# Local attention scores in stage 2: from one float32 product over 64 rows to two bf16 products over 128 rows, and silu with a bounded exponent

## The chip, the cores and the metric

The kernel runs on one core of a Trainium2 chip. The metric is the device time of one execution in microseconds, as the median of several runs. The profile is of one execution of its own. Engines are named as in the profile: PE (TensorE, with PEld for its weight loads), DVE (VectorE), ACT (ScalarE), POOL (GpSimd) and SP (SyncE, which issues the DMAs here).

## The reference

The program computes a block with gated linear attention, and on its result a second layer with three branches: an mLSTM branch, a local attention branch and a stick-breaking branch. Each branch is multiplied by silu of a gate. The change concerns the silus of the second layer and the scores of its local attention. Cut to that, the reference is:

```
def swa_branch(q, k, v, sinks):            # A_HEADS = 6, A_KV = 2, A_DH = 64, WINDOW = 128
    ...
    qb = q.reshape(B, nb, WINDOW, A_KV, G, A_DH)          # G = 3 query heads per key head
    kh = k.reshape(B, nb, WINDOW, A_KV, A_DH)
    kk = jnp.concatenate([jnp.concatenate([pad, kh[:, :-1]], 1), kh], 2)   # block before, own block
    scores = jnp.einsum('bnqkgd,bnskd->bnkgqs', qb, kk).astype(jnp.float32) * (A_DH ** -0.5)
    ...
    probs = jax.nn.softmax(jnp.concatenate([scores, sink], axis=-1), axis=-1)[..., :-1]

def hybrid_layer(...):
    h = rmsnorm_2(x, g_pre) * (1.0 + scale[:, None]) + shift[:, None]
    (mu, mv, mi, mf, mz, aq, ak, av, az, sq, sk, sv, sz) = jnp.split(h @ w_in, OFFSETS, axis=-1)
    y_m = mlstm_branch(mu, mv, ...) * jax.nn.silu(mz)     # with silu(causal_conv(u)) inside
    y_a = swa_branch(aq, ak, av, a_sinks) * jax.nn.silu(az)
    y_s = stickbreak_branch(sq, sk, sv) * jax.nn.silu(sz)
    ...
```

## The kernel before

The program has three stages. Stage 1 computes the first layer, 16 tiles of 128 tokens. Stage 2 (`mix_phase`) computes, for the same 16 tiles in order, the projections of the second layer, its mLSTM branch and its local attention, and writes the operands of the stick-breaking branch to memory. Stage 3 (`stick_phase`) computes that branch, the output product and the norm. Between stages all engines meet.

In stage 2 each engine runs its own list of instructions, written out by hand in the function `tile` of its block. Engines wait for each other by semaphores whose names say what is done (`aqk_done`, `aqk_copied`, `h_lo_done`). An engine works through its list in the order in which it is written; nothing is rearranged. The order of the lists and the PSUM bank that a product goes to therefore set all the timing.

The projections are float32 products in three bf16 ones: high times high, high times low, low times high (lines L1413, L1414, L1415). For tile i PE does in order: the forget and input gates and u (bank G0), mz (G1), then queries and keys `aq`, `ak` (G0, which must have been emptied of u by ACT, `u_copied`), the transposes of the probabilities and heads of tile i-1, v (G1), small products that turn the gate rows into columns (L1507 to L1510) and spread a row over 128 partitions (L1514, into bank B7, which DVE must have read for the heads of tile i-1, `ym_mid`), az (G0, which needs `aqk_copied`), the probabilities of tile i-1 times v (L1468), q and k of the mLSTM (L1528, L1529), sq and sk (G1), the mLSTM's own products, sz (G0), sv (G1), the intra-tile product (L1568) and last the scores of the local attention (L1584): 6 heads by 2 blocks of keys (one block in the first tile), each a float32 product over 64 rows, 128 queries by 128 keys. Then the next tile's gate products wait for `h_lo_done`.

ACT empties the banks. For each silu it copies the product to `z_sb` and takes the exponential of its negative to `e_sb` (`gate_out`, L1145 and L1146). When the last of the three, sz, is there, it takes the logarithm of 1 + e and the exponential of its negative over all 1024 columns (L1210, L1211). That is released as `silu_rec` to POOL, which multiplies it with `z_sb` (L1118). ACT goes on with the copy of sv (L1214) and the high half of the next tile's h (L1140, `h_hi_done`); DVE makes the low half (L1257, `h_lo_done`). DVE then goes straight on: numerators and denominators of the mLSTM (L1364 to L1373), scores plus bias (L1381), their maxima (L1385 to L1388). ACT takes the exponentials of the scores (L1229) and then, first in its list of the next tile, copies u out of G0 (L1165).

For the scores ACT copies the queries, scaled, and the keys as float32 from bank G0 (L1177, L1178). Keys of two tiles are kept. POOL computes the causal convolution with nine instructions (L1088 to L1094) and DVE in the same time the row chain of the gates with nine small ones (L1310 to L1319). The silu of the convolution is again three passes of ACT (L1183 to L1185) and a multiplication by DVE (L1327). In stage 1, ACT computes the silu of c for the second layer once, in its first tile (L352 to L356).

## Time and profile before

| | us |
|---|---|
| median of 3 runs | 2326.86 (2325.99 to 3398.17) |
| profiled execution, its own time | 2321.77 |
| its span | 2320.0 |

| engine | busy in the span | share |
|---|---|---|
| PE | 2118.8 us | 91% |
| DVE | 1422.6 us | 61% |
| ACT | 1111.8 us | 48% |
| POOL | 567.5 us | 24% |

Stage 1 takes the first 946 us or so, stage 2 the time to about 1770, stage 3 the rest. The shares are averages over the three stages; in stage 2 alone PE is busy nearly all the time. A matmul's record is longer than the time until the next one starts, so the cost of a row of products is read from start to start. On ACT and DVE, too, an instruction that waits for nothing can start before the record of the last one ends. A row in brackets says how long the engine was idle before it and who ended that.

### The profile page before, as it was taken

The numbers are of one execution on the slowest core, as the hardware profiler recorded it, in microseconds if no ns is written. First come the engines' busy times: TensorE is split into PE (matmuls) and PEld (weight loads), VectorE is DVE, ScalarE is ACT, GpSimd is POOL, SyncE is SP. The second block draws the span as 40 slices with busy tenths as digits, with TensorE's granted clock in tenths as the row PEclk, the third lists the DMA queues.
The fourth block names the chain that finished last, engine by engine and source line by source line (L and its number), as shares of the span: only waits on it lengthen the run. The fifth ranks groups of instructions, "written<-read, shape, count | busy, mean of one in ns | idle before, by whom it ended". The sixth has DMA issues, their size and how long they took to land. (4 is left out here: it accounts for less than half of the span.)

```text
span 2320.0 us, 48214 instructions
## 1 busy us (share of the span) xinstructions
PE 2118.8 (91%) x19996; PEld 1488.3 (64%) x19996; DVE 1422.6 (61%) x2478; ACT 1111.8 (48%) x2407; POOL 567.5 (24%) x554
## 2 busy tenths in 40 slices
PE   1699999999999998699999999999994698989887
PEld 1466666666666664599988999998992343434333
DVE  6755555555555553256665555666554798989885
ACT  2444444444444443234434334434333687978775
POOL 0520100000000100333343333344332232323221
PEclk9799999999999998899999999999996899999999
DMA  9422222223222224411001011001004312020111
GB/s 398 151 89 81 84 80 76 88 90 102 81 89 85 89 71 141 131 26 46 27 27 30 27 29 46 27 27 30 27 18 155 109 46 82 23 88 19 64 55 55
DMA packets 129962, 174.54 MB, mean 75 GB/s; under 512 B 46928, under 2 KB 98256, under 8 KB 127696
## 3 DMA queue, kind: packets, MB, share of 16 engines
q1 hardware_dynamic: 129456, 170.41, 22.8%
q8 instruction: 158, 2.59, 0.5%
q10 hardware_dynamic: 288, 1.05, 0.1%
q14 instruction: 60, 0.49, 0.1%
HBM read 122.39 MB, written 49.03 MB: 74 GB/s over the span
## 5 line engine op out<-in xcount | busy, mean ns | idle before, releaser
L1413 PE MATMUL m_bank<-h_hi,w_all 128*128 128x128 bf16 (+1 forms) x2560 | 437.5, 220 | 19.2 <-POOL m_arena L1041 17.7
L1415 PE MATMUL m_bank<-h_hi,w_all 128*128 128x128 bf16 (+1 forms) x2560 | 436.9, 220 | 0.1
L1414 PE MATMUL m_bank<-h_lo,w_all 128*128 128x128 bf16 (+1 forms) x2560 | 436.9, 220 | 0.0
L1413 PEld LDWEIGHTS m_bank<-h_hi,w_all 128*128 128x128 bf16 (+1 forms) x2560 | 251.5, 98 | 27.8 <-POOL m_arena L1041 18.2
L1414 PEld LDWEIGHTS m_bank<-h_lo,w_all 128*128 128x128 bf16 (+1 forms) x2560 | 251.7, 98 | 0.6 <-issue 0.2
L1415 PEld LDWEIGHTS m_bank<-h_hi,w_all 128*128 128x128 bf16 (+1 forms) x2560 | 251.7, 98 | 0.0
L1774 POOL TENSOR_TENSOR s_hi<-s_sp,s_cols 128x512 bf16<-128x512 f32 x144 | 152.3, 1057 | 352.9 <-DVE s_sp L1869 141.2
L283 POOL TENSOR_TENSOR g_stage<-g_stage,g_nh_row 128x1024 f32<-128x1024 f32 x16 | 52.3, 3272 | 736.0 <-DVE g_stage L617 736.0
L680 PE MATMUL g_bank<-w_all,h_hi 128*128 128x512 bf16 x512 | 194.2, 379 | 0.7 <-ACT g_stage L372 0.7
L681 PE MATMUL g_bank<-w_all,h_hi 128*128 128x512 bf16 x512 | 194.0, 379 | 0.0
L682 PE MATMUL g_bank<-w_all,h_lo 128*128 128x512 bf16 x512 | 194.0, 379 | 0.0
L680 PE MATMUL g_bank<-h_hi,w_all 128*128 128x128 bf16 x1024 | 175.3, 220 | 0.0
L681 PE MATMUL g_bank<-h_lo,w_all 128*128 128x128 bf16 x1024 | 175.1, 220 | 0.0
L682 PE MATMUL g_bank<-h_hi,w_all 128*128 128x128 bf16 x1024 | 175.0, 220 | 0.0
L1795 ACT ACTIVATE s_ar<-s_ar 128x512 f32<-128x512 f32 x144 | 89.6, 622 | 69.7 <-DVE s_ar L1880 69.6
L1942 PE MATMUL s_bank<-s_q,s_k_c 128*128 128x256 bf16 x576 | 89.6, 281 | 26.9 <-issue 13.7
L1880 DVE TENSOR_TENSOR s_ar<-s_zs,s_bank 128x512 f32<-128x512 f32 x144 | 98.4, 683 | 24.1 <-PE s_bank L1960 22.1
L1968 PE MATMUL s_bank<-s_ar,s_v_c 128*64 128x256 f32 x576 | 94.8, 408 | 14.0 <-ACT s_ar L1795 13.3
L1875 DVE TENSOR_TENSOR s_lo<-s_sp,s_hi 128x512 bf16<-128x512 f32 x144 | 99.2, 689 | 12.9 <-POOL s_hi L1774 12.9
L1791 ACT ACTIVATE s_ab<-s_ab,s_cols 128x512 f32<-128x512 f32 x144 | 104.2, 723 | 4.7
L680 PEld LDWEIGHTS g_bank<-h_hi,w_all 128*128 128x128 bf16 x1024 | 100.8, 98 | 1.8 <-issue 0.2
L1864 DVE SCALAR_TENSOR_TENSOR s_sp<-s_zs,s_ab 128x512 f32<-128x512 f32 x144 | 98.8, 686 | 3.7 <-ACT s_ab L1791 1.4
(349 smaller groups left out, 5295.8 us busy)
## 6 DMA issues: line engine op xcount, KB each, us to landing
g_piece<-in_w_dram SPq DMA_DIRECT2D x64, 268.0 KB, 3.3
g_stage<-in_gla_w_in_dram SPq DMA_DIRECT2D x8, 1552.0 KB, 12.4
g_stage<-in_ada_w_dram SPq DMA_DIRECT2D x8, 1536.0 KB, 11.3
g_piece<-in_w_mod_t_dram SPq DMA_DIRECT2D x48, 256.0 KB, 3.2
w_hi<-g_piece_hi SPq DMA_DIRECT2D x64, 134.0 KB, 2.0
w_lo<-g_piece_lo SPq DMA_DIRECT2D x64, 134.0 KB, 2.2
g_xs<-in_x_dram SPq DMA_DIRECT2D x16, 512.0 KB, 4.3
s_xr<-x SPq DMA_DIRECT2D x16, 512.0 KB, 4.1
```

Source lines behind the costliest of these rows:

```text
L680: pe.matmul(out, l_hi, r_hi, start=(k == 0), stop=False)
L681: pe.matmul(out, l_hi, r_lo, start=False, stop=False)
L682: ins = pe.matmul(out, l_lo, r_hi, start=False, stop=(k == n - 1))
L1413: pe.matmul(out, l_hi, r_hi, start=(k == 0), stop=False)
L1414: pe.matmul(out, l_hi, r_lo, start=False, stop=False)
L1415: ins = pe.matmul(out, l_lo, r_hi, start=False, stop=(k == n - 1))
L1774: pool.tensor_tensor(hi[k][:], sp_[k], one_col.broadcast_to([P, 512]), ALU.mult).then_inc(s["hi_done"], 1)
L1791: act.activation(ab[k], ab[k], ACT.Ln, bias=one_col).then_inc(s["ln_done"], 1)
L1864: ins = dve.scalar_tensor_tensor(sp_[k], zs[k][:], 0.0, ab[k], ALU.max, ALU.add)
L1875: dve.tensor_tensor(lo[k][:], sp_[k], hi[k][:], ALU.subtract).then_inc(s["lo_done"], 1)
L1880: dve.tensor_tensor(ar[k][:], zs[k][:], C[k % 2][:], ALU.subtract).then_inc(s["arg_done"], 1)
L1968: ins = pe.matmul(O[j * SD:(j + 1) * SD, k % 2 * T2:(k % 2 + 1) * T2], v_h, ar[k][:, j * T2:(j + 1) * T2], start=False, stop=True, skip_gr ...
```

## The change

Scores: the queries of each key head are kept in bf16 as one operand of 128 rows, 64 rows with the high half and 64 rows with the low half (what rounding left). The keys are kept in bf16 as two operands, high and low, each twice over, so that it has 128 rows too. A score is then the sum of two bf16 products over 128 rows: stacked queries times high keys, stacked queries times low keys. ACT makes the high halves (of the keys two copies), and signals `aqk_high`; DVE makes the low halves, after its row chain and ahead of the heads of the tile before, and signals `aqk_copied`. The heads are now worked in order, and the semaphore between head 2 and head 3 is gone.

Silu: exp(-z) becomes two instructions, Relu(z + 40) and exp(40 - that), which is exp(-max(z, -40)). In `gate_out` the Relu takes the place of the exponential that read the bank; a new pass over 1024 columns ahead of the logarithm is the exponential. The convolution and the silu of c each get one pass more. Two constants of 40.0 are set by POOL, one in stage 1 and one ahead of stage 2.

```diff
@@ stage 1
-                act.activation(e2, c2_row, ACT.Exp, scale=-1.0).then_inc(s["c2_link"], 1)
+                act.activation(e2, c2_row, ACT.Relu, bias=floor_col).then_inc(s["c2_link"], 1)
                 act.wait_ge(s["c2_link"], 1)
+                act.activation(e2, e2, ACT.Exp, scale=-1.0, bias=floor_col).then_inc(s["c2_link"], 1)
+                act.wait_ge(s["c2_link"], 2)
                 act.activation(e2, e2, ACT.Ln, bias=one_col).then_inc(s["c2_link"], 1)
@@ stage 2, buffers and constants
-        aq = carve3(AG, T)
-        ak, av = carve3(2, T), carve(AKV * AD)
+        q_st = carve(AKV * AG * T, BF16).rearrange("p (g n) -> p g n", g=AKV)
+        k_st = carve(2 * AKV * T, BF16).rearrange("p (s g t) -> p s g t", s=2, g=AKV)
+        k_lo = carve(2 * AKV * T, BF16).rearrange("p (s g t) -> p s g t", s=2, g=AKV)
+        av = carve(AKV * AD)
...
             pre(pool.memset(one_col, 1.0))
+            pre(pool.memset(floor_col, FLOOR))
@@ stage 2, ACT
-                act.activation(e_sb[0:n, at[0]:at[1]], bank[0:n, 0:at[1] - at[0]], ACT.Exp, scale=-1.0)\
+                act.activation(e_sb[0:n, at[0]:at[1]], bank[0:n, 0:at[1] - at[0]], ACT.Relu, bias=floor_col)\
                    .then_inc(s[name + "_read"], 1)
...
                 act.wait_ge(s["aqk_done"], i + 1)
                 wait("scores_done", i)
-                act.activation(aq.rearrange("p j t -> p (j t)"), G0[:, 0:AG * T], ACT.Copy, scale=AD ** -0.5)
-                act.activation(ak[:, par, :], G0[:, AG * T:AG * T + T], ACT.Copy).then_inc(s["aqk_copied"], 1)
+                for g in range(AKV):
+                    ps = slice(g * AD, (g + 1) * AD)
+                    act.activation(q_st[ps, g, :], G0[ps, 0:AG * T], ACT.Copy, scale=AD ** -0.5)
+                    for to in range(AKV):
+                        ins = act.activation(k_st[to * AD:(to + 1) * AD, par, g, :], G0[ps, AG * T:AG * T + T], ACT.Copy)
+                ins.then_inc(s["aqk_high"], 1)
                 if not first:
                     p_high(i - 1)
                 act.wait_ge(s["conv_done"], i + 1)
                 wait("cu_done", i)
-                link.done(act.activation(ec, cv, ACT.Exp, scale=-1.0))
+                link.done(act.activation(ec, cv, ACT.Relu, bias=floor_col))
+                link.done(act.activation(ec, ec, ACT.Exp, scale=-1.0, bias=floor_col))
                 link.done(act.activation(ec, ec, ACT.Ln, bias=one_col))
...
                 act.wait_ge(s["sz_read"], i + 1)
+                link.done(act.activation(e_sb, e_sb, ACT.Exp, scale=-1.0, bias=floor_col))
                 link.done(act.activation(e_sb, e_sb, ACT.Ln, bias=one_col))
@@ stage 2, DVE
                 dve.tensor_scalar(nM_r, m_r, -1.0, None, ALU.mult).then_inc(s["rows_done"], 1)
+                dve.wait_ge(s["aqk_high"], i + 1)
+                for g in range(AKV):
+                    ps, other = slice(g * AD, (g + 1) * AD), slice((1 - g) * AD, (2 - g) * AD)
+                    dve.scalar_tensor_tensor(q_st[other, g, :], G0[ps, 0:AG * T], AD ** -0.5, q_st[ps, g, :], ALU.mult, ALU.subtract)
+                    for to in (ps, other):
+                        ins = dve.tensor_tensor(k_lo[to, par, g, :], G0[ps, AG * T:AG * T + T], k_st[ps, par, g, :], ALU.subtract)
+                ins.then_inc(s["aqk_copied"], 1)
                 if not first:
                     heads_out(i - 1, 1 - par)
@@ stage 2, PE
-                for head in (0, 1, 2, 4, 5, 3):
-                    if head == 3:
-
-                        pe.wait_ge(s["head_2_scored"], i + 1)
+                for head in range(AH):
+                    g, j = head // AG, head % AG
+                    ps, js = slice(g * AD, (g + 1) * AD), slice(j * T, (j + 1) * T)
                     for half in range(1 if first else 0, 2):
                         slot = par if half else 1 - par
-                        g, j = head // AG, head % AG
-                        ps = slice(g * AD, (g + 1) * AD)
                         at = (head % 2) * 2 * T + half * T
-                        ins = pe.matmul((B3, B5, B6)[head // 2][:, at:at + T], aq[ps, j, :], ak[ps, slot, :],
-                                        start=True, stop=True)
-                    if head == 2:
-                        ins.then_inc(s["head_2_scored"], 1)
+                        bank = (B3, B5, B6)[head // 2][:, at:at + T]
+                        pe.matmul(bank, q_st[:, g, js], k_st[:, slot, g, :], start=True, stop=False)
+                        ins = pe.matmul(bank, q_st[:, g, js], k_lo[:, slot, g, :], start=False, stop=True)
```

On ACT, the list at the end of a tile, from the two readings of the sz product to the high half of h. Before:

```order
L1145 ACTIVATE m_arena<-m_bank 128x256
L1146 ACTIVATE m_arena<-m_bank 128x256
L1210 ACTIVATE m_arena<-m_arena,m_cols 128x1024
L1211 ACTIVATE m_arena<-m_arena 128x1024
L1214 ACTIVATE m_arena<-m_bank 128x256
L1140 ACTIVATE h_hi<-m_arena 128x1024
```

Of the change:

```order
L1152 ACTIVATE m_arena<-m_bank 128x256
L1153 ACTIVATE m_arena<-m_bank,m_cols 128x256
L1222 ACTIVATE m_arena<-m_arena,m_cols 128x1024
L1223 ACTIVATE m_arena<-m_arena,m_cols 128x1024
L1224 ACTIVATE m_arena<-m_arena 128x1024
L1227 ACTIVATE m_arena<-m_bank 128x256
L1147 ACTIVATE h_hi<-m_arena 128x1024
```

One instruction over 1024 columns is added, and the second reading of the bank has a bias column (`m_cols`) as a third operand.

On DVE, from the end of the row chain to the mask of the decay matrix. Before:

```order
L1318 SCALAR_TENSOR_TENSOR m_arena<-m_arena 4x128
L1319 TENSOR_SCALAR m_arena<-m_arena 4x128
L1268 SCALAR_TENSOR_TENSOR m_arena<-m_bank,m_cols,m_arena 128x128 x3
L1273 TENSOR_TENSOR m_arena<-m_arena 128x384
L1291 TENSOR_TENSOR m_arena<-m_bank,m_arena 128x2x128 x3
L1327 TENSOR_TENSOR m_arena<-m_arena 128x384
L1333 SCALAR_TENSOR_TENSOR m_arena<-m_bank,m_cols,m_maskneg 128x128 x4
```

Of the change:

```order
L1331 SCALAR_TENSOR_TENSOR m_arena<-m_arena 4x128
L1332 TENSOR_SCALAR m_arena<-m_arena 4x128
L1336 SCALAR_TENSOR_TENSOR m_arena<-m_bank,m_arena 64x384
L1338 TENSOR_TENSOR m_arena<-m_bank,m_arena 64x128 x2
L1336 SCALAR_TENSOR_TENSOR m_arena<-m_bank,m_arena 64x384
L1338 TENSOR_TENSOR m_arena<-m_bank,m_arena 64x128 x2
L1281 SCALAR_TENSOR_TENSOR m_arena<-m_bank,m_cols,m_arena 128x128 x3
L1286 TENSOR_TENSOR m_arena<-m_arena 128x384
L1304 TENSOR_TENSOR m_arena<-m_bank,m_arena 128x2x128 x3
L1347 TENSOR_TENSOR m_arena<-m_arena 128x384
L1353 SCALAR_TENSOR_TENSOR m_arena<-m_bank,m_cols,m_maskneg 128x128 x4
```

Six instructions (L1336, L1338) stand between the row chain and the heads of the tile before (L1268, now L1281). Nothing else on DVE changes its place.

## Rows read from the trace of the kernel before

**Rows 1.** PEld in order of time (start us, us, engine, line): query products.

```profile
1108.30 0.10 PEld L1413 LDWEIGHTS m_bank<-h_hi,w_all 128*128 128x128 bf16 x1 [0.22 <-ACT m_arena L1165]
...
1158.11 0.10 PEld L1413 LDWEIGHTS m_bank<-h_hi,w_all 128*128 128x128 bf16 x1 [0.21 <-ACT m_arena L1165]
```

**Rows 2.** Stretch in stage 2: us, busy PE PEld DVE ACT POOL, clock, DMA.

```profile
1200.00:1300.00 100.00, 99.91 (x1345) 90.77 (x1343) 59.56 (x118) 41.22 (x120) 38.22 (x38) 1.00 0.11 31
```

**Rows 3.** Waits in stage 2 (960 to 1770): us in total, times, longest.

```profile
PEld m_bank L1413 <- ACT m_arena L1165: 3.0, 14, 0.2
```

**Rows 4.** ACT in order of time, one boundary between tiles.

```profile
1092.45 1.15 ACT L1210 ACTIVATE m_arena<-m_arena,m_cols 128x1024 f32<-128x1024 f32 x1
1093.63 1.06 ACT L1211 ACTIVATE m_arena<-m_arena 128x1024 f32<-128x1024 f32 x1
...
1095.30 0.39 ACT L1214 ACTIVATE m_arena<-m_bank 128x256 f32<-128x256 f32 x1 [0.61 <-PE m_bank L1415]
...
1107.77 0.48 ACT L1165 ACTIVATE m_arena<-m_bank 128x384 f32<-128x384 f32 x1
```

**Rows 5.** DVE in order of time, the low half of h, same boundary.

```profile
1096.66 1.55 DVE L1257 TENSOR_TENSOR h_lo<-m_arena,h_hi 128x1024 bf16<-128x1024 f32 x1 [4.93 <-ACT h_hi L1140]
```

**Rows 6.** PE in order of time, same boundary: scores, gate products, u products.

```profile
1096.06 2.60 PE L1584 MATMUL m_bank<-m_arena 64*128 64x128 f32 x24
...
1098.59 0.23 PE L1413 MATMUL m_bank<-h_hi,w_all 128*36 128x128 bf16 x1
...
1100.04 0.23 PE L1413 MATMUL m_bank<-h_hi,w_all 128*128 128x128 bf16 x1
...
1104.02 0.22 PE L1415 MATMUL m_bank<-h_hi,w_all 128*128 128x128 bf16 x1
```

**Rows 7.** PE in order of time, the boundary after the first tile.

```profile
1000.33 0.23 PE L1413 MATMUL m_bank<-h_hi,w_all 128*36 128x128 bf16 x1 [0.72 <-DVE h_lo L1257]
```

**Rows 8.** ACT in order of time, copies of queries and keys, and of v.

```profile
1113.87 0.49 ACT L1177 ACTIVATE m_arena<-m_bank 128x384 f32<-128x384 f32 x1 [3.92 <-PE m_bank L1415]
1114.26 0.27 ACT L1178 ACTIVATE m_arena<-m_bank 128x128 f32<-128x128 f32 x1
...
1120.70 0.49 ACT L1188 ACTIVATE m_arena<-m_bank 128x384 f32<-128x384 f32 x1 [0.90 <-PE m_bank L1415]
```

**Rows 9.** POOL in order of time: after sz, and in the convolution.

```profile
1094.77 2.36 POOL L1118 TENSOR_TENSOR m_arena<-m_arena 128x1024 f32<-128x1024 f32 x1 [5.55 <-ACT m_arena L1211]
...
1111.77 1.00 POOL L1091 TENSOR_TENSOR m_arena<-m_arena 128x384 f32<-128x384 f32 x1
...
1117.20 0.82 POOL L1094 TENSOR_TENSOR m_arena<-m_arena,m_cols 128x384 f32<-128x384 f32 x1
```

**Rows 10.** DVE in order of time, softmax and row chain.

```profile
1108.33 1.76 DVE L1283 TENSOR_TENSOR m_arena<-m_arena,m_cols 128x1536 f32<-128x1536 f32 x1
...
1111.99 0.91 DVE L1312 TENSOR_TENSOR m_arena<-m_arena 4x128 f32<-4x128 f32 x1
```

**Rows 11.** DVE in order of time, heads of the tile before, and decay mask.

```profile
1117.34 0.87 DVE L1268 SCALAR_TENSOR_TENSOR m_arena<-m_bank,m_cols,m_arena 128x128 f32<-128x128 f32 x3
...
1123.17 1.13 DVE L1333 SCALAR_TENSOR_TENSOR m_arena<-m_bank,m_cols,m_maskneg 128x128 f32<-128x128 f32 x4 [2.11 <-ACT m_cols L1197]
```

**Rows 12.** PE in order of time, the products into the heads' bank.

```profile
1121.54 0.69 PE L1514 MATMUL m_bank<-m_arena,m_sel 4*128 4x128 f32 x4
```

**Rows 13.** DVE in stage 1, first tile, silu of c.

```profile
109.79 1.56 DVE L589 TENSOR_TENSOR w_all<-w_all,g_piece 128x1024 f32<-128x1024 f32 x1 [5.48 <-ACT g_piece L356]
```

**Rows 14.** DVE in the last tile, scores plus bias.

```profile
1747.06 1.89 DVE L1381 TENSOR_TENSOR m_arena<-m_bank,m_arena 128x512 f32<-128x512 f32 x3 [0.55 <-PE m_bank L1584]
```

**Rows 15.** PE in stage 3, after idle times.

```profile
2041.23 0.39 PE L1959 MATMUL s_bank<-s_hi,s_tri 128*128 128x512 bf16 x1 [1.90 <-DVE s_lo L1875]
...
2167.70 0.61 PE L1959 MATMUL s_bank<-s_hi,s_tri 128*128 128x512 bf16 x1 [3.18 <-DVE s_lo L1875]
```

**Rows 16.** Stretch at stage 2's start, after 17.7 us of idle PE.

```profile
951.60:955.40 3.80, 3.73 (x35) 3.55 (x36) 0.00 (x0) 0.00 (x0) 3.39 (x6) 0.50 0.23 43
```

More of the change, by code:

```diff
@@ L28 @@
 TAU = 16.0
+FLOOR = 40.0
 GA = 32
@@ L114, in gla_phase @@
         mod_part, b2_col, gp2_col = cols[:, 96:96 + N_MOD], cols[:, 144:168], cols[:, 168:176]
-        h_scale_2, h_shift_2 = cols[:, 176:184], cols[:, 184:192]
+        h_scale_2, h_shift_2, floor_col = cols[:, 176:184], cols[:, 184:192], cols[:, 192:193]
         piece = sb("piece", [P, 2 * W2P])
@@ L266, in _ @@
             pool.memset(one_col, 1.0).then_inc(s["pool_pre"], 1)
-            pool.wait_ge(s["pool_pre"], 6)
+            pool.memset(floor_col, FLOOR).then_inc(s["pool_pre"], 1)
+            pool.wait_ge(s["pool_pre"], 7)
             pool.affine_select(out=ident[:], in_=ident[:], compare_op=ALU.not_equal, fill=1.0, base=0,
@@ L274, in _ @@
                                pattern=[[1, T]], channel_multiplier=-1).then_inc(s["pool_pre"], 1)
-            pool.wait_ge(s["pool_pre"], 9)
+            pool.wait_ge(s["pool_pre"], 10)
             for h in range(GH):
@@ L351, in c2_silu @@
                 act.wait_ge(s["c2_in"], 16)
[L352 removed]
+                act.activation(e2, c2_row, ACT.Relu, bias=floor_col).then_inc(s["c2_link"], 1)
                 act.wait_ge(s["c2_link"], 1)
+                act.activation(e2, e2, ACT.Exp, scale=-1.0, bias=floor_col).then_inc(s["c2_link"], 1)
+                act.wait_ge(s["c2_link"], 2)
                 act.activation(e2, e2, ACT.Ln, bias=one_col).then_inc(s["c2_link"], 1)
[L355 removed]
+                act.wait_ge(s["c2_link"], 3)
                 act.activation(e2, e2, ACT.Exp, scale=-1.0).then_inc(s["c2_link"], 1)
@@ L587, in tile @@
                 if first:
-                    dve.wait_ge(s["c2_link"], 3)
+                    dve.wait_ge(s["c2_link"], 4)
                     dve.tensor_tensor(c2_row, c2_row, piece[:, 0:D], ALU.mult).then_inc(s["c2_ready"], 1)
@@ L910, in mix_phase @@
         gp_col, h_scale = col(8), col(8)
-        eps_col, one_col, ssx, lnx, rsx = col(1), col(1), col(1), col(1), col(1)
+        eps_col, one_col, floor_col, ssx, lnx, rsx = (col(1) for _ in range(6))
         cw_col, cb_col, hn_col, sk_col = col(TAPS * MB), col(MB), col(MB), col(MB)
@@ L920, in mix_phase @@
         G0, G1, TR, B3, B4, B5, B6, B7 = banks
-        names = ("w_zeroed consts_in pool_pre consts_ready bias_ready scale_ready gate_out "
+        names = ("w_zeroed aqk_high consts_in pool_pre consts_ready bias_ready scale_ready gate_out "
                  "x_stat xn_done xT_done hf_done h_hi_done h_lo_done "
@@ L929, in mix_phase @@
                  "rows_done silu_rec silu_done p_link sqk_split ym_out ya_out sq_out sk_out sv_out sz_out dve_pre act_pre dve_link act_link "
-                 "head_2_scored").split()
+                 ).split()
         sem = phase_semaphores(nc, ctx, "m_")
@@ L1145, in gate_out @@
                 act.activation(z_sb[par][0:n, at[0]:at[1]], bank[0:n, 0:at[1] - at[0]], ACT.Copy)
-                act.activation(e_sb[0:n, at[0]:at[1]], bank[0:n, 0:at[1] - at[0]], ACT.Exp, scale=-1.0)\
+                act.activation(e_sb[0:n, at[0]:at[1]], bank[0:n, 0:at[1] - at[0]], ACT.Relu, bias=floor_col)\
                    .then_inc(s[name + "_read"], 1)
-            ACT_LINKS = 9
+            ACT_LINKS = 11
             def p_high(i):
```

1 line of the change is left out of this document (removed).

## The prediction

> **What bounds the kernel now.** I read the stretches first, then who waits for whom, then one tile instruction by instruction. Stage 2, where the change lies, is 16 tiles of 128 tokens that repeat to the hundredth: the ScalarE copy that releases the query and key products ends the same way in every tile, and the weight load behind it comes every 49.81 us (1108.30 to 1158.11 [rows 1]). In 100 us of this stage PE is busy for 99.91, at a granted clock of 1.00, while DVE has 59.56 and ACT 41.22 [rows 2]. That looks like a stage which only PE bounds, and a change that shortens PE's work would be gain for gain. The waits say otherwise. In 14 tiles PE waits about 0.2 us for the copy of u [rows 3]. It is short, but it is a wait on another engine in each round, so a closed loop through ACT and DVE already sets the period, and PE's own work fits in it with 0.2 us to spare.
>
> The loop, in one round: the products for sz end; ACT copies and takes exponential, logarithm and exponential of 1024 columns, copies sv, makes the high half of the next h; DVE makes its low half (L1257), then without a pause numerators, scores plus bias, maxima; ACT takes six exponentials (the group at L1229) and copies u (L1165, 1107.77); PE may overwrite G0 with the queries and keys (1108.30) [rows 1, 4, 5]. From there to the next sz PE runs without a wait. So the period is PE's stretch from queries to sz, which the change leaves alone, plus this chain. I cost the change by what it does to the chain.
>
> **PE: the scores.** Now 12 products over 64 rows in float32 take from 1096.06 to the first gate product at 1098.59, 2.53 us [rows 6]. The new code has 24 bf16 products of 128x128 moving 128. The like of these stands beside them: 72 of them from 1100.04 to 1104.02, 0.056 us each [rows 6]. So 24 x 0.056 = 1.34 us, 1.19 us less. What follows the scores is not PE's: the gate products wait for the low half of h, and DVE's use of the scores stands behind L1257 and the numerators in its own queue. In the first tile, which has half the scores, PE stood for 0.72 us before the gates until L1257 was done [rows 7]: that is where the 1.19 us go. I credit them with nothing.
>
> **ACT: the sz chain.** The second reading of the bank becomes Relu with a bias column. A bias column costs 0.09 us, if it is that which sets L1210 (1.15 us, with one) apart from L1211 (1.06, without; the one is a logarithm, the other an exponential) [rows 4]. Then comes one more exponential over 1024 columns with a bias; from the start of L1210, which has the same form, to that of L1211 is 1.18 us [rows 4]. Together the reciprocal is done 1.27 us later. ACT itself has 0.61 us of idle time ahead of L1214, and gains 0.1 more because an instruction that waits for nothing starts before the last one ends (L1178 starts at 1114.26, L1177 ends at 1114.36 [rows 8]): sv and the high half of h come 1.27 - 0.61 - 0.1, some 0.55 us later.
>
> **DVE against POOL.** It is here that I choose. The same reciprocal releases POOL's multiplication of 1024 columns (L1118, 1094.77 to 1097.13), and DVE's L1257, from 1096.66 to 1098.21, has two SBUF inputs [rows 5, 9]. DVE does 1536 columns of this kind in 1.76 us, but takes 0.91 us for a small step of 128 (L1312, from 1111.99) beside POOL's L1091, which runs from 1111.77 to 1112.77; DVE ends 0.13 behind it [rows 9, 10]. By the 1536 columns, 1024 would need some 1.2 us; it takes 1.55, and ends 1.08 after POOL. So I take it that L1257 stands until L1118 is through. With L1118 1.27 us later (1096.04 to 1098.40) and L1257 ready at 1097.21, L1257 ends at 1098.40 + 1.08 = 1099.48: 1.27 us later than now, not 0.55. The Trainium skill ("SBUF — State Buffer", section "Who interferes with whom") has the rule for it: a VectorE instruction with two SBUF inputs and a GpSimd instruction that reads SBUF exclude each other, and the later one stands for the whole of the other. By that rule the sum is 21 us, without it 10; this trace agrees with it, by the 0.91 us and the 0.13 behind POOL.
>
> All that DVE and ACT do up to L1165 follows without a pause, so the copy of u and with it the period move by 1.27 us. There are 15 boundaries between tiles: 15 x 1.27 = 19.1 us. PE starts the gates at 1099.53 instead of 1098.59, stands there some 2.0 us (its scores end at 1097.4 and drain 0.15 later) and again 0.22 + 1.27 - 0.94 = 0.55 us for the copy of u.
>
> **Keys and queries, for nothing.** ACT copies in six pieces of 64 rows instead of two: 384 columns cost 0.39 from start to start (1113.87, 1114.26), 128 columns 0.27 less the overlap of 0.1 [rows 8], so 2 x (0.39 + 2 x 0.17) = 1.46 instead of 0.56 us. ACT's conv chain waits for POOL's L1094, which ends at 1118.02 [rows 9], and covers that; the chain's own extra pass of 384 columns, 0.49 us and a little for the bias, fits into the 0.90 us of idle time ahead of the copy of v at 1120.70 [rows 8]. DVE gets six new instructions behind the row chain, each PSUM and SBUF in: a piece of 128 columns costs 0.29 (three in 0.87), one of 512 some 0.6 (three in 1.89), so one of 384 about 0.49, and the block 2 x (0.49 + 2 x 0.29) = 2.1 us [rows 11, 14]. Behind it are queued the outputs of the heads: they end at 1118.2 now and at 1120.3 then, and PE wants their bank at 1121.54 [rows 11, 12]. 1.2 us are left. The keys and queries are done at 1119.4, before the products for az, which come behind those at 1121.54. The 2.11 us of idle time ahead of L1333 [rows 11] are used up by it, to the last tenth. If the cover at the heads' bank were gone, each us of the block beyond 2.1 + 1.2 = 3.3 would cost 15 us.
>
> **Once.** Stage 1 has the same extra pass in its first tile, with DVE waiting 5.48 us for its end, and PE behind [rows 13]: 1.27 us. POOL sets one more constant before stage 2's first products, which wait for it; I take 0.2 us, and at most the 0.91 of a small step that stands. In the last tile DVE waits 0.55 us for the scores [rows 14], which now come early; a chain that is 1.27 later uses that up: + 0.7. Sum: 19.1 + 1.3 + 0.2 + 0.7 = **+21.2 us**. The profiled execution, 2321.77 us (span 2320.0), would take 2343.0. The median of the runs is 2326.86, 5.1 above it; against it the forecast is **2348 us**, 0.9% slower, which is less than the 2% (46.5 us) that a measurement of this kernel can tell from no change.
>
> **Rivals.**
> *Only ACT's delay counts* (15%). If L1257 does not stand for L1118, the period grows by 0.55: 15 x 0.55 + 1.3 + 0.2 + 0 = 9.8, 2337 us. Against it speaks the 1.55 us of L1257.
> *The clock falls at the new gap* (12%). A gap of 1.90 us was followed by a 512-column product of 0.39 us, one of 3.18 us by one of 0.61 [rows 15]; 2.0 lies beside the first. After a long idle time PE ran 3.8 us at 0.50 [rows 16], the lower of its two levels, 1.2 GHz, which loses 1.9 us. PE would come to the queries at 1108.08 + 0.94 + 1.9 = 1110.92, 1.35 us after the copy of u: 15 x 2.62 + 2.1 = 41, 2368 us, 1.8% slower.
> *DVE's new block is slow: slower than before by over 2%* (5%). If each of its six instructions took the 0.91 us of L1312 [rows 10], it would last 5.5 us. The heads' outputs would be late from 3.3 us on, PE would stand 2.2 us at 1121.54 in 15 tiles, 33 us: 21 + 33 = 54, 2381 us. Against it: L1268 has one input in PSUM, one in SBUF, and ran at 0.29 a piece from 1117.34 on while POOL's L1094 was in progress from 1117.20 [rows 9, 11]. The Trainium skill's page "SBUF — State Buffer" ("Who interferes with whom") asks for two SBUF inputs, which these don't have; by it too the block stays at 2.1.
> *PE's saving comes through* (6%). It needs the chain to have slack that I don't see; 16 x 1.19 = 19 less, and 1.5 for the single costs: 2309 us, 0.8% faster.
> The forecast's case has 52%; 10% are for mixtures and for what I have not seen, half of them above it.
>
> **Range and chances.** From 2333 (below the second case, for a cheaper bias) to 2369 (with the clock case in it); outside lie the saving, the slow block and some of the mixtures, near 18%. Faster by over 2% 1%, within 2% 92%, slower by over 2% 7% (the slow block, and a falling clock with anything added).
>
> **What would show it.** In the changed trace: weight loads behind L1165's successor 51.1 us apart; scores 1.34 us long; PE idle for some 2 us ahead of the gates with DVE's low half as the cause; the POOL multiplication 1.27 us later against sz, the low half of h ending 1.1 us behind it; PE's clock 1.00 after the gap; DVE's block of six 2.1 us and no wait at the heads' bank. A period of 50.4 us says the second case, one of 52.4 the clock, a wait of PE for the heads' outputs the third. If the period stayed at 49.8 or fell, my loop is wrong.

## The result, and the profile after

| | changed kernel | kernel before, same chip |
|---|---|---|
| median | 2345.39 us (2344.33 to 2348.76, 4 runs) | 2326.43 us (2325.75 to 3398.17, 4 runs) |
| ratio | 1.0089, 95% interval 1.0077 to 1.0102 | |
| profiled execution, its own time | 2348.76 us | 2321.77 us |
| its span | 2347.0 us | 2320.0 us |
| PE, DVE, ACT, POOL busy | 2108.2, 1473.7, 1166.6, 564.2 us | 2118.8, 1422.6, 1111.8, 567.5 us |

The forecast was 2348 us, 0.9% slower; measured were 2345.4 and 0.9%. PE has 10.6 us less work and the kernel takes 19 us more. One run of the kernel before, 3398.17 us, lies far above its other three (2325.75 to 2326.86); why is not known, and the ratio leaves it out. The profiled execution of the changed kernel is the slowest of its four, that of the kernel before lies below all four of its runs, so the two traces differ by 27.0 us of span, and the account below has to fill 27.0, not 19.0.

A stretch of 100 us in stage 2 of the changed kernel, to be set beside [rows 2] (us; busy PE, PEld, DVE, ACT, POOL; clock, DMA):

```profile
1200.00:1300.00 100.00, 95.16 (x1316) 86.10 (x1315) 64.80 (x126) 47.18 (x128) 36.47 (x37) 1.00 0.11 31
```

PE was busy for 99.91 of 100 us and is now for 95.16, at the same clock. The waits of stage 2 (us in total, times, longest) say for whom it stands at the boundaries between tiles; before there were only the line of [rows 3] and 0.7 us for the low half, once, in the first tile:

```profile
PEld m_bank L1433 <- DVE h_lo L1270: 34.0, 15, 2.9
PE m_bank L1433 <- DVE h_lo L1270: 31.4, 15, 2.7
PEld m_bank L1433 <- ACT m_arena L1172: 5.9, 11, 0.5
```

One boundary between two tiles, engine by engine. ACT in order of time, from the two readings of the sz product to the high half of h, and the copy of u behind the softmax (answers to [rows 4]):

```profile
1203.72 0.47 ACT L1153 ACTIVATE m_arena<-m_bank,m_cols 128x256 f32<-128x256 f32 x1
1204.22 1.15 ACT L1222 ACTIVATE m_arena<-m_arena,m_cols 128x1024 f32<-128x1024 f32 x1
1205.40 1.15 ACT L1223 ACTIVATE m_arena<-m_arena,m_cols 128x1024 f32<-128x1024 f32 x1
1206.58 1.06 ACT L1224 ACTIVATE m_arena<-m_arena 128x1024 f32<-128x1024 f32 x1
1207.55 0.37 ACT L1227 ACTIVATE m_arena<-m_bank 128x256 f32<-128x256 f32 x1
1207.81 1.05 ACT L1147 ACTIVATE h_hi<-m_arena 128x1024 bf16<-128x1024 f32 x1
...
1220.71 0.47 ACT L1172 ACTIVATE m_arena<-m_bank 128x384 f32<-128x384 f32 x1
```

The new exponential (L1222) costs 1.18 us from start to start, and the copy of sv (L1227) has no idle time ahead of it any more: the 0.61 us are used up. POOL and DVE at the same place (answers to [rows 9] and [rows 5]):

```profile
1207.72 2.35 POOL L1125 TENSOR_TENSOR m_arena<-m_arena 128x1024 f32<-128x1024 f32 x1 [6.82 <-ACT m_arena L1224]
```

```profile
1208.89 2.26 DVE L1270 TENSOR_TENSOR h_lo<-m_arena,h_hi 128x1024 bf16<-128x1024 f32 x1 [5.47 <-ACT h_hi L1147]
1211.07 0.55 DVE L1384 TENSOR_TENSOR m_arena<-m_bank,m_cols 128x388 f32<-128x388 f32 x1
```

POOL waits 6.82 us for the reciprocal, 1.27 more than the 5.55 of [rows 9]. DVE's low half is ready only 0.54 later than before (5.47 against 4.93), but it lasts 2.26 us instead of 1.55 and ends at 1211.15, 1.08 behind POOL's end at 1210.07. From here on this is called the lock: DVE's instruction stands while POOL's runs. PE, same boundary, the last of the 24 scores products (the first starts at 1207.65) and the first gate product (answers to [rows 6]):

```profile
1207.65 0.22 PE L1602 MATMUL m_bank<-m_arena 128*128 128x128 bf16 x1
...
1208.93 0.22 PE L1603 MATMUL m_bank<-m_arena 128*128 128x128 bf16 x1
1211.20 0.23 PE L1433 MATMUL m_bank<-h_hi,w_all 128*36 128x128 bf16 x1 [2.05 <-DVE h_lo L1270]
```

The scores take 24 slots of 0.056 us, 1.34, and PE then stands 2.05 us. The first weight load for queries in this tile and the next (answers to [rows 1]):

```profile
1221.24 0.10 PEld L1433 LDWEIGHTS m_bank<-h_hi,w_all 128*128 128x128 bf16 x1 [0.54 <-ACT m_arena L1172]
...
1272.30 0.10 PEld L1433 LDWEIGHTS m_bank<-h_hi,w_all 128*128 128x128 bf16 x1 [0.54 <-ACT m_arena L1172]
```

They are 51.06 us apart, before 49.81: 1.25 us more in each round. DVE behind the row chain, the six new instructions and the heads (answers to [rows 11]):

```profile
1230.83 0.55 DVE L1336 SCALAR_TENSOR_TENSOR m_arena<-m_bank,m_arena 64x384 bf16<-64x384 f32 x1
1231.40 0.58 DVE L1338 TENSOR_TENSOR m_arena<-m_bank,m_arena 64x128 bf16<-64x128 f32 x2
1231.99 0.56 DVE L1336 SCALAR_TENSOR_TENSOR m_arena<-m_bank,m_arena 64x384 bf16<-64x384 f32 x1
1232.57 0.60 DVE L1338 TENSOR_TENSOR m_arena<-m_bank,m_arena 64x128 bf16<-64x128 f32 x2
1233.20 0.87 DVE L1281 SCALAR_TENSOR_TENSOR m_arena<-m_bank,m_cols,m_arena 128x128 f32<-128x128 f32 x3
```

PE comes to the heads' bank 0.41 us after their end at 1234.07, and without a wait (answers to [rows 12]):

```profile
1234.48 1.13 PE L1534 MATMUL m_bank<-m_arena,m_sel 4*128 4x128 f32 x8
```

**The account of 27.0 us.** I take the starts of DVE's low half as marks.

| stretch | before | after | more | of it |
|---|---|---|---|---|
| to the first product of stage 2 | 951.66 | 954.10 | 2.44 | stage 1 2.29, POOL's constant 0.15 |
| from there to the first low half | 47.07 | 48.54 | 1.47 | high half later 0.54; a pause of PE 0.93 |
| 14 intervals between low halves | 697.35 | 717.95 | 20.60 | 14 x 1.26 = 17.6; clock 3.0 |
| last low half to stage 3's first product | 82.79 | 84.08 | 1.29 | the low half longer 0.71; the last tile 0.58 |
| stage 3, not touched | | | 1.2 | open |

The starts of the low half cut the first and the last of the 15 boundaries: 0.54 of the first lies in the second row of the table, 0.71 of the last in the fourth. With them the 15 boundaries cost 0.54 + 17.64 + 0.71 = 18.9 us, 1.26 each.

The 0.93 us of the second row are not the change's own (`e5_u_early` and `e7_all_three` below have the new silu and scores and no such pause). In the first tile PE pauses once without a wait that the profile shows:

```profile
970.56 0.22 PE L1434 MATMUL m_bank<-h_lo,w_all 128*128 128x128 bf16 x1 [1.24 <-issue]
```

From start to start it loses 1.4 us there; the kernel before loses 0.5, in two short pauses. `e11_stage1_back` below, with the very same stage 2, has an idle time of 0.54 us there and takes 47.81 us for this row. Across the kernels the idle time lies between nothing and 2.12 us; why is open.

In the changed kernel the granted clock fell in 4 of the 14 intervals (they last 50.97, the first, which would be 49.38, and 52.07 to 52.11 instead of 51.07); before in one (51.45 for 49.81). In the changed kernel each of the four falls begins right behind the gap ahead of the gates, 0.2 to 1.2 us after PE starts again. One such stretch:

```profile
1058.00:1060.00 2.00, 2.00 (x22) 2.00 (x20) 1.97 (x5) 1.68 (x10) 0.00 (x0) 0.50 0.06 18
```

PE runs there at 0.50, the lower of its two levels. A fall costs 1.6 us where nothing covers it, and 1.04 where the wait of 0.5 for u would have followed anyway.

The fall in the kernel before is of another kind. It begins 25 us after the gate products, with no idle time of PE beside it, behind the small products that turn gate rows into columns and spread a row (L1507, L1510, L1514; the last of the three, and a stretch behind it):

```profile
1520.07 1.13 PE L1514 MATMUL m_bank<-m_arena,m_sel 4*128 4x128 f32 x8
```

```profile
1522.20:1524.20 2.00, 2.00 (x22) 2.00 (x20) 0.64 (x3) 0.63 (x1) 0.00 (x0) 0.50 0.00 0
```

PE was busy all through at a clock of 1.00 until then. So a longer interval alone does not say that a gap let the clock fall; one has to look where in the tile the stretch at 0.50 begins.

### The profile page after: what moved, and what is told of

It is laid out like the page before. It is cut to its first block and busy times, and to the rows that moved or that the text cites. A ratio compares the mean times of both kernels' runs of the same rounds, so it can differ in the third digit from the quotient of the medians.

```text
span 2347.0 us, 48409 instructions
## 1 busy us (share of the span) xinstructions
PE 2108.2 (90%) x19996; PEld 1476.2 (63%) x19996; DVE 1473.7 (63%) x2574; ACT 1166.6 (50%) x2504; POOL 564.2 (24%) x556
```

## The experiments

The period is the distance between two starts of DVE's low half in tiles whose clock did not fall. The gap is PE's idle time ahead of the gate products (in the first tile, which has half the scores, it is longer by half their time; where the table has 2.05 it is 2.72 there). Falls are counted in the 14 intervals of one trace, in two columns: those that begin right behind the gap, and those that begin behind the small products, 25 us later. Ratios are to the kernel before on the same chip.

| kernel | period | gap | falls behind the gap | falls behind the small products | median | ratio, 95% interval |
|---|---|---|---|---|---|---|
| before | 49.81 | 0 | 0 | 1 | | |
| the change | 51.07 | 2.05 | 4 | 0 | 2345.39 | 1.0089 (1.0077 to 1.0102) |
| e1, scores only | 49.81 | 0.79 | 0 | 4 | 2322.56 | 0.9990 (0.9982 to 0.9999) |
| e2, silu only | 51.07 | 0.86 | 0 | 1 | 2346.29 | 1.0090 (1.0077 to 1.0102) |
| e3, POOL late | 50.03 | 1.02 | 0 | 1 | 2328.20 | 1.0010 (1.0000 to 1.0020) |
| e4, scores twice | 51.07 | 0.72 | 1 | 1 | 2347.87 | 1.0095 (1.0080 to 1.0110) |
| e5, u early | 50.53 | 2.05 | 6 | 0 | 2345.75 | 1.0094 (1.0081 to 1.0107) |
| e6, POOL late, exponential behind h | 49.54 | 0.52 | 0 | 1 | 2317.95 | 0.9978 (0.9968 to 0.9988) |
| e7, all three | 49.00 | 0.52 | 0 | 2 | 2311.55 | 0.9945 (0.9933 to 0.9957) |
| e8, kernel before with all three | 49.60 | 0 | 0 | 1 | 2326.16 | 1.0018 (1.0001 to 1.0035) |
| e9, u early, scores twice | 50.53 | 0.72 | 0 | 3 | 2338.55 | 1.0047 (1.0034 to 1.0061) |
| e10, all three, h ahead of sv | 48.76 | 0.28 | 0 | 2 | 2309.55 | 0.9932 (0.9918 to 0.9945) |
| e11, stage 1 as before | 51.07 | 2.05 | 2 | 0 | 2341.55 | 1.0074 (1.0059 to 1.0088) |

### Each half of the change alone

`e1_scores_only` takes the silu back everywhere:

```diff
-                link.done(act.activation(e_sb, e_sb, ACT.Exp, scale=-1.0, bias=floor_col))
                 link.done(act.activation(e_sb, e_sb, ACT.Ln, bias=one_col))
...
-  bank[0:n, 0:at[1] - at[0]], ACT.Relu, bias=floor_col)
+  bank[0:n, 0:at[1] - at[0]], ACT.Exp, scale=-1.0)
```

> The change with its silus put back to three passes: the scores are the two bf16 products, with the six copies of ACT and the six small DVE instructions. Theory (the period is set by the loop sz, ACT, low half of h, DVE, ACT's copy of u): 2326 us, between 2323 and 2329, with a period of 49.8 us; PE's 1.19 us go into a gap of 0.8 us ahead of the gates. Rival (PE bounds the stage): 2307 us, period 48.6. Rival (the new copies on ACT and DVE are late for someone): over 2332.

Measured: 2322.56 us, just under the 2323 to 2329 expected, and a period of 49.81 to the hundredth. The scores' shorter stretch became PE's wait for the low half (waits of stage 2):

```profile
PE m_bank L1429 <- DVE h_lo L1266: 12.6, 15, 1.5
PE m_bank L1429 <- ACT m_arena L1170: 5.2, 14, 0.4
```

12.6 us in 15 boundaries are 0.84 each (0.79 in all but the first). So 1.19 us of work were taken from PE in every tile and the tile got no shorter: crediting them with nothing was right.

`e2_silu_only` keeps the new silu and takes the scores back to float32 with their old buffers and copies.

> The change with its scores put back to float32: only the silus are bounded. Theory: the whole loss is here, 15 x 1.27 and 1.5 us more, 2345 us, or some 3 us less because PE's gap ahead of the gates is only 1.0 us and the clock then does not fall (it fell in 4 of 15 gaps of the change); period 51.07, DVE's low half of h 2.26 us long. Rival (part of the loss comes with the scores): 2335 or less.

Measured: 2346.29 us, the whole loss of the change. The low half of this kernel:

```profile
1209.46 2.27 DVE L1264 TENSOR_TENSOR h_lo<-m_arena,h_hi 128x1024 bf16<-128x1024 f32 x1 [5.47 <-ACT h_hi L1145]
```

The loss is all the silu's, with or without the new scores: of the 1.26 us in each round, 0.54 are the high half coming later and 0.72 the low half lasting longer. The 3 us that a steadier clock was to give back were not seen in the median. In the trace the 14 intervals do take 3.0 us less than in the change (714.95 for 717.95), but the first tile takes 2.7 more: PE's pause there lasts 2.12 us, and the clock falls behind it.

### POOL's multiplication moved away from the low half

`e3_pool_late` lets POOL multiply only when the maxima of the scores are there, long behind DVE's low half:

```diff
                 pool.wait_ge(s["silu_rec"], i + 1)
+                pool.wait_ge(s["max_done"], i + 1)
                 pool.tensor_tensor(z_sb[par], z_sb[par], e_sb, ALU.mult)
```

> The change, with POOL's multiplication of 1024 columns held back until DVE has the maxima of the scores; nothing else is moved. Theory (DVE's low half of h stands while that multiplication runs): the low half takes 1.22 us instead of 2.26, the loop is 0.55 - 0.33 = 0.22 us longer than in the kernel before, period 50.0; 2331 us, between 2328 and 2335. Rival (only ACT's delay counts and POOL is without effect): 2345 as the change.

Measured: period 50.03 for 50.0 expected, median 2328.20 for 2331. POOL and DVE of this kernel, each in order of time, in one tile:

```profile
1209.79 2.54 POOL L1126 TENSOR_TENSOR m_arena<-m_arena 128x1024 f32<-128x1024 f32 x1 [15.83 <-DVE m_cols L1409]
```

```profile
1201.96 1.23 DVE L1271 TENSOR_TENSOR h_lo<-m_arena,h_hi 128x1024 bf16<-128x1024 f32 x1 [5.47 <-ACT h_hi L1148]
```

With the same 5.47 us of idle time ahead, the same instruction takes 1.23 us with POOL 6.6 us away and 2.26 beside it. That is the lock, shown by moving the one partner: 1.04 us a tile. One line of code leaves 3.3 us over the kernel before on the same chip, where the silu alone cost 21.4. In the kernel before, too, the instruction took 1.55.

### More work for PE

`e4_scores_twice` computes each score twice, 24 more products a tile:

```diff
-                        pe.matmul(bank, q_st[:, g, js], k_st[:, slot, g, :], start=True, stop=False)
-                        ins = pe.matmul(bank, q_st[:, g, js], k_lo[:, slot, g, :], start=False, stop=True)
+                        for _again in range(2):
+                            pe.matmul(bank, q_st[:, g, js], k_st[:, slot, g, :], start=True, stop=False)
+                            ins = pe.matmul(bank, q_st[:, g, js], k_lo[:, slot, g, :], start=False, stop=True)
```

> The change, with each pair of score products done twice over, 24 more products, 1.34 us more for PE in each tile. Theory (PE has a gap of 2.2 us there): no loss; 2345 us, or some 3 us less where the shorter gap of 0.9 us keeps the clock up (in the change it fell in 4 of 15 gaps at about 1 us each). Rival (PE's time counts): 2345 + 16 x 1.34 = 2366.

Measured: 2347.87 us, the same ratio as the change's within the intervals; the period is 51.07 as before it, and the gap shrinks by the 1.3 us that the products take:

```profile
PE m_bank L1433 <- DVE h_lo L1270: 12.1, 15, 2.1
```

PE's work ahead of the gates is free up to the width of the gap. The gain of some 3 us from a steadier clock, which I had hoped for, was not seen: the trace has two falls instead of four, but each costs 1.6 now instead of 1.04. One of the two begins behind the first tile's gap, which is still 2.05 us long; behind the 14 gaps of 0.72 none begins.

### The copy of u ahead of the softmax: a miss

`e5_u_early` has ACT copy u out of G0 before the exponentials of the scores, not behind them:

```diff
+                if not last:
+                    copy_u(i + 1)
                 act.wait_ge(s["max_done"], i + 1)
                 act.activation(es, es, ACT.Exp)
```

> The change, with ACT's copy of u moved from behind the six exponentials of the scores to ahead of them, into ACT's wait for the maxima. PE then need not wait for it. Theory (the wait of 0.53 us at the queries is part of the period): what is left is the loop over the low half of h, 51.06 - 0.53 = 50.53 us, so 2345 - 8 = 2337 us; PE's wait for the copy of u is gone, the wait ahead of the gates stays near 2.2 us. Rival (the wait is made up elsewhere, since POOL's convolution starts 3 us earlier and stands in DVE's way): 2345 or more.

Expected were 2337 us, measured 2345.75, no gain at all. The period did what was said: 50.53, 0.54 less, and the wait for u is gone. But 6 of the 14 intervals are longer, five by 1.5 to 1.6 us and the first by 2.8 (49.38 in its twin below). All six falls begin right behind the gap, within 0.6 us, and yet the gap ahead of the five is the same as in tiles without a fall:

```profile
1209.39 0.23 PE L1439 MATMUL m_bank<-h_hi,w_all 128*36 128x128 bf16 x1 [2.05 <-DVE h_lo L1276]
1261.49 0.23 PE L1439 MATMUL m_bank<-h_hi,w_all 128*36 128x128 bf16 x1 [2.05 <-DVE h_lo L1276]
1312.02 0.29 PE L1439 MATMUL m_bank<-h_hi,w_all 128*36 128x128 bf16 x1 [2.05 <-DVE h_lo L1276]
1364.09 0.23 PE L1439 MATMUL m_bank<-h_hi,w_all 128*36 128x128 bf16 x1 [2.05 <-DVE h_lo L1276]
```

From the first to the second 52.10 us, then 50.53, then 52.07. In the change the 0.54 us of waiting for u took up a third of each fall; without that wait every fall counts in full. 13 x 0.54 = 7.0 us won, and 10.6 lost to the clock where the change lost 1.6 + 3 x 1.04 = 4.7: a net gain of 1.1 us is left in the traces (716.8 for 717.95 in all 14), and nothing in the medians. So the clock has to be reckoned with after all, which the next kernel tries.

`e9_u_early_scores_twice` is `e5_u_early` with the doubled products of `e4_scores_twice`.

> The change with the copy of u early (as e5_u_early) and with each pair of score products done twice (as e4_scores_twice). In e5_u_early the period of an undisturbed tile fell to 50.53 us as forecast, but in 6 of 15 tiles PE's clock fell at the gap of 2.2 us and the tile took 1.6 us more. Theory (it is PE's idle time ahead of the gates that lets the clock fall): 24 more products shorten the gap to 0.9 us, the clock falls in 2 tiles or fewer, the period stays 50.53, and more work for PE gives 2338 to 2341 us, 5 to 8 below e5_u_early. Rival (the gain of e5_u_early was lost elsewhere, or the clock falls by chance whatever the gap): 2345 us, or 2345 + 21 if PE's time counts.

Measured: 2338.55 us, as expected, and a ratio of 1.0047, against 1.0094 of `e5_u_early`; the two intervals don't touch. The same place in this kernel:

```profile
1158.62 0.23 PE L1439 MATMUL m_bank<-h_hi,w_all 128*36 128x128 bf16 x1 [0.72 <-DVE h_lo L1276]
1209.16 0.23 PE L1439 MATMUL m_bank<-h_hi,w_all 128*36 128x128 bf16 x1 [0.72 <-DVE h_lo L1276]
```

The period is the same 50.53, the gap 0.72 instead of 2.05. Three falls are left where two or fewer were expected, and none of them begins behind the gap: all three begin behind the small products, as the one in the kernel before does. Shortening the gap did away with the falls behind it, and falls of the other kind came. A kernel with 372 more products is faster by 7 us; in the traces the clock takes 3 x 1.6 = 4.9 us for 10.6, 5.7 less. By the ratios the two kernels lie 0.0047, some 11 us, apart, so about half of that is accounted for. They ran on different chips, each beside the kernel before, and one trace of each shows the falls, so the rest stays open.

### Shortening the loop

`e6_pool_late_sz_split` is `e3_pool_late` with the last exponential of the sz chain moved behind the copy of sv and the high half of h; POOL, its only reader, waits longer anyway.

```diff
-                act.activation(e_sb, e_sb, ACT.Exp, scale=-1.0).then_inc(s["silu_rec"], 1)
                 act.wait_ge(s["sv_done"], i + 1)
                 wait("sv_out", 16 * i)
                 act.activation(sv, G1[:, 0:SW], ACT.Copy).then_inc(s["sv_copied"], 1)
                 if not last:
                     h_high(i + 1)
+                act.activation(e_sb, e_sb, ACT.Exp, scale=-1.0).then_inc(s["silu_rec"], 1)
```

> The change, with POOL's multiplication held back as in e3_pool_late, and the last of ACT's three passes over 1024 columns put behind the high half of h. Theory (loop as in the kernel before, less the 0.33 us that the low half of h stood there): period 49.5, 2326 - 5 + 1.5 = 2323 us. Rival (three passes cannot be hidden, whatever their order): 2328 as e3_pool_late.

Measured: period 49.54 for 49.5, median 2317.95, 5 us under the 2323 expected. Two of the 5 are the chip: the expectation starts from 2326 us, and the kernel before takes 2323.91 here. The other three stay open.

`e7_all_three` adds the early copy of u of `e5_u_early`.

> The change with all three moves: POOL's multiplication late, the last pass behind the high half of h, the copy of u early. Theory: the loop is now PE from the gates to sv (46.3 us), 1.36 us to the end of the high half, 1.22 for the low half: period 48.9, 2326 - 13 + 1.5 = 2314 us. Rival (the moves don't add up; DVE and POOL collide in the softmax): 2323 as e6_pool_late_sz_split.

Measured: 49.00 for 48.9, 2311.55 for 2314. The copy of u, whose 0.54 us a tile brought nothing to the median in `e5_u_early`, takes 0.55 us a tile and 6 us off the median here.

`e8_before_three` makes the same three edits on the kernel before, so that it and `e7_all_three` differ by the change alone.

> The kernel before (float32 scores, silus in three passes) with the same three moves. Theory: PE's own work bounds it, 49.81 - 0.22 = 49.6 us, 2323 us, so that here the bf16 scores of e7_all_three are worth some 9 us, which they are not in the change itself. Rival (the scores are worth nothing in either): equal to e7_all_three or below it by the 1.5 us of the single costs.

Measured: period 49.60 as expected, but the runs scatter from 2317.02 (the profiled one) to 2338.54, so the median of 2326.16, 2 us above the kernel before, says little; why these runs scatter so stays open. PE waits for the low half once in 15 boundaries (0.5 us in all): this kernel is bound by PE's own work. The periods say what the change is worth once the loop is short: 49.60 - 49.00 = 0.6 us a tile, 9 us, about half of the 1.19 us that the scores save.

`e10_h_before_sv` takes `e7_all_three` and has ACT make the high half of h ahead of the copy of sv:

```diff
+                if not last:
+                    h_high(i + 1)
                 act.wait_ge(s["sv_done"], i + 1)
                 wait("sv_out", 16 * i)
                 act.activation(sv, G1[:, 0:SW], ACT.Copy).then_inc(s["sv_copied"], 1)
-                if not last:
-                    h_high(i + 1)
                 act.activation(e_sb, e_sb, ACT.Exp, scale=-1.0).then_inc(s["silu_rec"], 1)
```

> e7_all_three with ACT's copy of sv put behind the high half of h, both of which wait for the same product. Theory (the loop is PE from the gates to sv, high half, low half): 0.28 us less in each round, period 48.7 us, 15 x 0.28 = 4 below e7_all_three, near 2308 us. Rival (PE's own work bounds e7_all_three at 49.0): no difference.

Measured: period 48.76, 0.24 less for 0.28, median 2309.55 for 2308, 0.7% under the kernel before. It is the lowest median of all, though the interval of its ratio overlaps that of `e7_all_three`. DVE's low half and PE's gap in it:

```profile
1195.70 1.22 DVE L1277 TENSOR_TENSOR h_lo<-m_arena,h_hi 128x1024 bf16<-128x1024 f32 x1 [4.74 <-ACT h_hi L1148]
```

```profile
1196.98 0.23 PE L1440 MATMUL m_bank<-h_hi,w_all 128*36 128x128 bf16 x1 [0.28 <-DVE h_lo L1277]
```

0.28 us of idle time are left per tile: the next step would have to shorten PE's own work.

### The single cost in stage 1

`e11_stage1_back` is the change with the silu of c in stage 1 as before.

```diff
-                act.activation(e2, c2_row, ACT.Relu, bias=floor_col).then_inc(s["c2_link"], 1)
-                act.wait_ge(s["c2_link"], 1)
-                act.activation(e2, e2, ACT.Exp, scale=-1.0, bias=floor_col).then_inc(s["c2_link"], 1)
+                act.activation(e2, c2_row, ACT.Exp, scale=-1.0).then_inc(s["c2_link"], 1)
```

> The changed kernel with the silu of c in stage 1 as it was before (three passes of ACT, not four); stage 2 as changed. It asks why stage 2 starts 2.4 us later and not the 1.5 of the forecast. Theory A: the fourth pass lengthens PE's idle time at the transposes from 1.45 to 2.38 us, and the clock falls behind it (0.91 in the stretch 112 to 130, 1.00 before), which adds some 1 us to the 1.27 of the pass. Without the pass: idle time 1.4 to 1.6 us, granted clock 1.00 in that stretch, and from the start of DVE's multiplication for c (L593 then, at about 109.8) to the first product of stage 2 842.0 us as before, not 843.4; median about 2.3 us under the changed kernel, 2343. Rival B: the clock there has nothing to do with the pass; it reads 0.91 again, the distance stays near 843.4, and only the pass itself, 1.2 us, comes back, 2344.2. The period of stage 2 is 51.07 by both. The two medians are close to what five rounds can tell apart; the trace decides.

Measured: 2341.55 us, 3.8 under the change where 2.3 were expected; the intervals of the two ratios overlap, so the trace has to decide. PE's idle time in stage 1's first tile and the clock behind it, first in the change:

```profile
114.71 0.92 PE L787 MATMUL g_bank<-g_ident,g_stage 128*128 128x128 f32 x4 [2.38 <-DVE g_stage L548]
...
112.00:130.00 18.00, 15.62 (x110) 10.36 (x109) 11.39 (x20) 7.47 (x18) 13.43 (x12) 0.91 0.29 101
```

and in `e11_stage1_back`:

```profile
113.98 0.66 PE L785 MATMUL g_bank<-g_ident,g_stage 128*128 128x128 f32 x4 [1.23 <-DVE g_stage L546]
...
112.00:130.00 18.00, 16.57 (x151) 12.09 (x150) 12.10 (x20) 8.99 (x20) 14.81 (x13) 1.00 0.27 91
```

Without the pass the gap is 1.23 us, the clock stays at 1.00, and stage 2's first product comes 841.84 us after the start of DVE's multiplication for c: the 842.0 of theory A, not the 843.4 of B. All nine traces with the pass have a gap of 2.38 to 3.24 us there and a clock of 0.91 or 0.81; all four without it have 1.23 to 1.73 and 1.00.

## Why the prediction was right

**The loop, and what bounds it: right.** The period was to be set by ACT's and DVE's chain and not by PE. `e1_scores_only` and `e4_scores_twice` change PE's work by -1.19 and +1.34 us a tile and leave the period as it was.

**The sz chain, 1.27: right.** POOL waits 1.27 us longer for it, and ACT's own delay of the high half is 0.54 for the 0.55 forecast.

**The lock, the step where I chose: right.** The forecast had the low half end 1.08 behind POOL, as before; it ends 1.08 behind. The alternative, 0.55 a boundary, 2337 us, fell with the period of 51.07. `e3_pool_late` shows the cause. The Trainium skill ("SBUF — State Buffer", section "Who interferes with whom") states this exclusion for a VectorE instruction with two SBUF inputs beside GpSimd; by it the trace and that run agree, 2.26 us beside POOL, 1.23 alone.

**15 boundaries of 1.27, 19.1 us: right.** Measured 15 x 1.26 = 18.9.

**The gaps:** 2.0 us forecast ahead of the gates, 2.05 measured; 0.55 at the queries, 0.54 measured; scores 1.34, as forecast.

**DVE's block: too small by 0.24.** 2.34 us for 2.1: an instruction of 384 columns over 64 rows takes 0.57 from start to start, and two of 128 columns 0.59. The heads end 0.41 us ahead of PE's need, not 1.2, because a step with two SBUF inputs in DVE's own list (L1296, 2.44 us for the 1.76 of [rows 10]) now also stands beside POOL's convolution (before, it was POOL's first step there that stood, L1088 with 2.45 us for some 0.83). The cover held, by little. It cost nothing. ACT's six copies took 2.02 us for the 1.46 forecast, likewise covered: the copy of v still has 0.41 us of idle time ahead of it.

**Once: too small by a clock fall.** 2.44 us to the start of stage 2 for the 1.5 forecast. ACT's three passes, 3.22 us from the first start to the start of what follows them, became four in 4.49, the 1.27 forecast; but PE's idle time grew by only 0.93 of it (1.45 to 2.38) and behind that longer gap the clock fell (`e11_stage1_back`). I had priced the wait of PE and not what follows it. The end was sized well, 0.58 for 0.7. The step by which it comes is this one: in the last tile too a step of DVE now stands beside POOL's sz multiplication (L1389, four columns, two SBUF inputs), and takes 1.26 us more; DVE's wait for the scores behind it is gone:

```profile
1770.41 1.57 DVE L1389 SCALAR_TENSOR_TENSOR m_cols<-m_arena 128x4 f32<-128x4 f32 x1
1772.02 0.17 DVE L1390 TENSOR_TENSOR m_cols<-m_cols 128x4 f32<-128x4 f32 x1
```

POOL's instruction runs there from 1769.62 to 1771.97, and L1389 takes 1.57 us where it took 0.31.

**The rival of the falling clock: in part true.** It was put as all or nothing, a fall in each of 15 tiles at 1.35 us, 2368 us. The clock fell behind 4 of the 15 gaps, and a fall in stage 2 was cheaper than the one of [rows 16]: some 3.3 us at 0.50, 1.6 us lost, 1.04 behind the wait for u. The gap of 1.90 in [rows 15], behind which nothing happened, was one case and could not show a chance of one in four. The forecast also says that stage 2 repeats to the hundredth; in the trace it was read from, one interval of 14 was 51.45 instead of 49.81, by a fall behind the small products, so a clock that falls now and then belonged to the kernel before.

**The sum.** Its own terms come to 18.9 + 1.3 + 0.2 + 0.6, near the 21.2 forecast. The pair of traces is 27.0 apart because of what the sum leaves out: 1.0 for the clock in stage 1, 3.0 for the clock in stage 2, 0.9 for PE's pause in the first tile, 1.2 in stage 3. The medians are 19.0 apart, less than the sum. The two profiled executions lie unevenly in their groups, that of the kernel before 4.7 us below its median, that of the changed kernel 3.4 above. How many falls and pauses the executions without a trace have isn't known, so that the forecast met the median to 3 us is partly luck: the clock was worth as much as that.

**PE's saving comes through: wrong here,** as `e1_scores_only` shows, and right in another kernel: where the loop is shortened, half of it does (`e7_all_three` against `e8_before_three`, 0.6 us a tile).

## What to carry to other kernels

An engine that is busy for 99.9% of a stage need not bound it: a wait of 0.2 us that returns in every round shows the loop that does, and what is added to that loop is paid in full while what is taken from the busy engine is not. When a pass is added on one engine, ask which instruction of a third engine it moves, and beside whose it then runs; here 1.27 us on ACT became 1.27 in the loop only through POOL, and moving POOL's multiplication gave most of it back. A new gap on PE has a second price, a clock that may fall behind it, and a gain of half a microsecond a tile can vanish in that. Before a fall is put down to a gap, look where in the tile it begins.

## What the runs showed of the hardware

- Behind PE's idle time ahead of the gates, the clock fell to 0.50 in 13 of 47 cases where it had lasted 2.05 to 2.72 us (the change 4 of 15, `e5_u_early` 6 of 15, `e11_stage1_back` 2 of 15, the first tiles of `e4_scores_twice` and `e9_u_early_scores_twice` 1 of 2), and in none of 120 where it had lasted 0.28 to 1.98 us (all other gaps there, of ten kernels). Equal gaps of 2.05 us don't have equal effects; what sets one apart from the next isn't known. A fall costs 1.6 us, once 2.8.
- The clock also falls while PE is busy: in the ten kernels without gaps of 2.05 us in every tile it fell in 19 of 150 tiles (each kernel's first tile left out) behind the small products of L1507 to L1514, the stretch at 0.50 beginning 2.0 to 2.6 us after the start of the last group. In the three kernels with those gaps it never fell there, in 45 tiles.
- More PE work went with a faster kernel: 24 more products a tile, in a gap, and 2338.55 instead of 2345.75 us (`e9_u_early_scores_twice`), on another chip, and with no falls behind that gap. Put into the change itself, where a fall behind the gap costs only 1.04 us, the same products changed nothing (`e4_scores_twice`).
- DVE with two SBUF inputs ended 1.08 us behind POOL both in the kernel before and in the changed one, though it had been ready at different times; the part that it does after POOL's end is nearly the whole instruction (1.23 us alone). Its instructions with one input in PSUM kept their time beside POOL: three pieces of 512 columns took 1.88 us beside POOL's L1074 and L1076 (L1304 at 1234.58) and 1.89 with POOL idle [rows 14]. The six new instructions were not put to that test, since POOL stood idle from 1230.72 to 1234.74.
